# Hybrid decoder step, two layers: input projections on unnormalised activations, and the next layer's splits in the gate loop

## The reference, cut to what matters

```python
def rms_norm(x, w):
    y = x32 * lax.rsqrt(jnp.mean(x32 * x32, axis=-1, keepdims=True) + EPS)
    return y * w

xn = rms_norm(h, norm_pre_mix)
proj = xn @ w_in
hq, hf, hi, hg, aq, ak, av, gq, gk, gv, g_lr, gr = jnp.split(proj, split_points, axis=-1)
...  # HGRN2, GLA (log_a from g_lr @ gla_w_gate2 + gla_b_gate), rotary attention
h = h + rms_norm(mix, norm_post_mix)
h = h + rms_norm(u @ w_down, norm_post_mlp)
h = h + jax.nn.sigmoid(h @ w_ple_gate) * (p_i @ w_ple)
```

## Time and profile before

| | |
|---|---|
| median of 3 runs | 1826.89 us |
| profiled execution, span | 1825.8 us |
| TensorE matmul / weight load | 1719.3 / 1601.2 us busy |
| VectorE / ScalarE / GpSimd | 841.6 / 652.6 / 71.2 us busy |
| DMA | 303.67 MB, mean 166 GB/s |

### The profile page before, as it was taken

How to read it: one execution, slowest core, us unless ns; L and a number is a source line. 1 busy time by engine, 2 the same in 40 slices (tenths; PEclk the granted TensorE clock), 3 DMA queues, 4 the chain that set the end, 5 groups by cost and what they waited for, 6 DMA issues and landing times.

```text
span 1825.8 us, 35764 instructions
## 1 busy us (share of the span) xinstructions
PE 1719.3 (94%) x16070; PEld 1601.2 (88%) x16070; DVE 841.6 (46%) x1311; ACT 652.6 (36%) x963; POOL 71.2 (4%) x90
## 2 busy tenths in 40 slices
PE   6999888899999999999979998888999999999988
PEld 5988775598999999998979887756989999999988
DVE  5413775535413333336554147754364243333365
ACT  5422324544423122233354232254443231322333
POOL 0011110000000000000000121100000000000000
PEclk9999898999999999999989998999999999999999
DMA  6511519931936636442354223398329266355311
GB/s 261 192 58 59 177 53 391 359 136 59 345 105 219 221 100 210 150 150 70 107 180 139 69 89 126 123 378 315 122 88 344 87 222 216 135 174 178 126 59 64
DMA packets 60649, 303.67 MB, mean 166 GB/s; under 512 B 7120, under 2 KB 8784, under 8 KB 58832
## 3 DMA queue, kind: packets, MB, share of 16 engines
q1 hardware_dynamic: 53072, 200.91, 30.8%
q0 software_dynamic: 7424, 100.47, 15.7%
HBM read 290.74 MB, written 111.08 MB: 220 GB/s over the span
## 4 chain that ended last, share of the span: by engine, by line
PE 85%; DVE 8%; ACT 3%; DMA 2%; issue 2%; SPq 0%; DVEq 0%; ACTq 0%
PE pair L1728 15%; PE pair L1730 15%; PE pair L1729 15%; PE pair L764 2%; PE pair L746 2%; PE pair L748 2%; PE pair L747 2%; PE pair L696 2%; PE pair L766 2%; PE pair L768 2%; PE pair L697 2%; PE pair L698 2%; DMA arena<-cv 2%; PE pair L1053 2%; PE pair L1808 2%
## 5 line engine op out<-in xcount | busy, mean ns | idle before, releaser
L1728 PE MATMUL pair<-x_hi_part,w_hi_part 128*128 128x288 f32 x1088 | 322.2, 296 | 2.1 <-DVE tmp L2107 2.1
L1729 PE MATMUL pair<-x_lo_part,w_hi_part 128*128 128x288 f32 x1088 | 321.0, 295 | 0.0
L1730 PE MATMUL pair<-x_hi_part,w_lo_part 128*128 128x288 f32 x1088 | 319.9, 294 | 0.0
L2044 DVE TENSOR_TENSOR w_lo_part<-raw,w_hi_part 128x1024 fp32r<-128x1024 f32 x154 | 188.7, 1225 | 237.9 <-ACT w_hi_part L1895 237.9
L1728 PE MATMUL pair<-u_hi_part,w_hi_part 128*128 128x288 f32 x928 | 274.7, 296 | 0.0
L1729 PE MATMUL pair<-u_lo_part,w_hi_part 128*128 128x288 f32 x928 | 273.8, 295 | 0.0
L1730 PE MATMUL pair<-u_hi_part,w_lo_part 128*128 128x288 f32 x928 | 272.8, 294 | 0.0
L1895 ACT ACTIVATE w_hi_part<-raw 128x1024 fp32r<-128x1024 f32 x154 | 161.9, 1051 | 212.6 <-PE pair L1730 208.3
L1728 PEld LDWEIGHTS pair<-x_hi_part,w_hi_part 128*128 128x128 f32 x1088 | 203.9, 187 | 2.5 <-DVE tmp L2107 2.5
L1730 PEld LDWEIGHTS pair<-x_hi_part,w_lo_part 128*128 128x128 f32 x1088 | 204.9, 188 | 0.0
L1729 PEld LDWEIGHTS pair<-x_lo_part,w_hi_part 128*128 128x128 f32 x1088 | 204.3, 188 | 0.0
(11 more groups left out here) (284 smaller groups left out, 3414.2 us busy)
## 6 DMA issues: line engine op xcount, KB each, us to landing
raw<-w_units SPq DMA_DIRECT2D x210, 512.0 KB, 3.5
ck_out<-ck POOLq DMA_DIRECT2D x16, 3060.0 KB, 14.1
arena<-cv SPq DMA_DIRECT2D x24, 640.0 KB, 9.6
arena<-ck SPq DMA_DIRECT2D x18, 640.0 KB, 10.7
more<-ck SPq DMA_DIRECT2D x18, 640.0 KB, 13.1
tail<-cv SPq DMA_DIRECT2D x18, 640.0 KB, 9.2
h<-ck SPq DMA_DIRECT2D x12, 640.0 KB, 12.7
y_out<-h SPq DMA_DIRECT2D x16, 288.0 KB, 2.1
```

The lines of the kernel that those rows point to most:

```text
L1728: nc.tensor.matmul(out, wh[:, cols], xh[:, k, t], start=n == 0, stop=False)
L1729: nc.tensor.matmul(out, wh[:, cols], xl[:, k, t], start=False, stop=False)
L1730: mm = nc.tensor.matmul(out, wl[:, cols], xh[:, k, t], start=False, stop=n == KT - 1)
L2044: return tt_(dst, src, hi.bitcast(F32), ALU.subtract).then_inc(*up(done, 1))
```

## The change

The products of IN1 and IN2 and of V are taken of h * weight, without RS, and the factor of each token is applied where PSUM is emptied: VectorE evicts IN1 and multiplies by RSP (the new name of RS, in a tile of its own), ScalarE evicts V with a scale for each token from a small tile RSTOK; hg and gr are multiplied in place by GpSimd (`pre_scale`), aq and ak through the rotary tables, which GpSimd multiplies by RSP.

The sum of squares moves on TensorE from ahead of the products to the seventh of their steps (`s == KT - 2`), with five one-column products for RSTOK, and into pair 3. In layer 0 GpSimd squares the tiles instead of ScalarE, while ScalarE and VectorE split them; the startup loads are put in another order. The first two weight units of a layer (`FIRST = 2`) have places of their own and are split outside the layer's queues: for layer 0 between its tiles, for layer 1 in the last two turns of layer 0's gate loop, where the tiles of the new h are split too (`next_hi`, `next_lo`). A tile's remainder lies where h was, so it waits for the store of that tile (`h_saved`, now two semaphores). SP loads units 4 to 7 of a layer ahead of the states, and the reset mask of the scans comes by a load of its own into the arena. The rotary tables are loaded anew for layer 1. At the end of layer 1 no squares are made any more.

Its core:

```diff
+FIRST = 2
+SPLIT = list(range(FIRST, R_PLE)) + list(range(R_UP, UNITS))
...
+            return pair[3 if name == "sum_pre" else 2 if name in APART else Q[name] % 2]
...
+            sp.dma_start(par[:, :], params[0]).then_inc(*up(s_par0, 16))
+            first_unit(0)
+            pair_of_tiles(0)
+            pair_of_tiles(1)
+            first_unit(1)
+            pair_of_tiles(2)
+            pair_of_tiles(3)
+            first_unit(2)
             sp.dma_start(con[:, 0:C_COS], consts[:, 0:C_COS]).then_inc(*up(s_con, 16))
             sp.dma_start(con[:, C_SCALE:C_END], consts[:, C_SCALE:C_END]).then_inc(*up(s_con, 16))
-            sp.dma_start(par[:, :], params[0]).then_inc(*up(s_par0, 16))
-            for i in range(RAW):
-                sp.dma_start(raw_sb[:, i * 1024:(i + 1) * 1024], w_first[0, i * P:(i + 1) * P, :]).then_inc(*up(s_w0[i], 16))
+            first_unit(3)
...
+        def next_hi(act, k):
+            nc.scalar.activation(NH[:, k], H[:, k], ACT.Copy, scale=par[:, W_PRE + k:W_PRE + k + 1]).then_inc(*up(xn_hi, 1))
+        def next_lo(dve, k, at_layer):
+            dve.wait_ge(xn_hi, KT * at_layer + k + 1)
+            nc.vector.scalar_tensor_tensor(NL[:, k], H[:, k], par[:, W_PRE + k:W_PRE + k + 1], NH[:, k].bitcast(F32),
+                                           ALU.mult, ALU.subtract).then_inc(*up(xn_split, 1))
+        def first_hi(act, i, at_layer):
+            act.wait_ge(s_w0[i], 16 * (at_layer + 1))
+            nc.scalar.activation(win_sb[3 + i][:, 0:1024], raw_sb[:, i * 1024:(i + 1) * 1024], ACT.Copy).then_inc(*up(w0_hi, 1))
+        def first_lo(dve, i, at_layer):
+            dve.wait_ge(w0_hi, FIRST * at_layer + i + 1)
+            nc.vector.tensor_tensor(win_sb[3 + i][:, 1024:2048], raw_sb[:, i * 1024:(i + 1) * 1024],
+                                    win_sb[3 + i][:, 0:1024].bitcast(F32), ALU.subtract).then_inc(*up(w0_split, 1))
+        def add_square(dve, k, at_layer, squares):
+            dve.wait_ge(sq_pre, KT * at_layer + k + 1)
+            if k >= 2:
+                dve.wait_ge(acc_pre, (KT - 1) * at_layer + k - 1)
+            nc.vector.tensor_tensor(RSP, squares(0) if k == 1 else RSP, squares(k), ALU.add).then_inc(*up(acc_pre, 1))
+        @block.gpsimd
+        def _(pool):
+            for k in range(KT):
+                if k % 2 == 0:
+                    pool.wait_ge(s_x[k // 2], 16)
+                nc.gpsimd.tensor_tensor(SQ_FIRST[:, k], H[:, k], H[:, k], ALU.mult).then_inc(*up(sq_pre, 1))
+        @block.scalar
+        def _(act):
+            nc.scalar.preload_act_table_set("natural_log_exp_and_others")
+            act.wait_ge(s_par0, 16)
+            for k in range(KT):
+                if k == 0:
+                    first_hi(act, 0, 0)
+                if k % 2 == 0:
+                    act.wait_ge(s_x[k // 2], 16)
+                next_hi(act, k)
+                if k == 3:
+                    first_hi(act, 1, 0)
+        @block.vector
+        def _(dve):
+            dve.wait_ge(s_par0, 16)
+            first_lo(dve, 0, 0)
+            for k in range(KT):
+                dve.wait_ge(sq_pre, k + 1)
+                next_lo(dve, k, 0)
+                if k == 3:
+                    first_lo(dve, 1, 0)
+                if k >= 1:
+                    add_square(dve, k, 0, lambda j: SQ_FIRST[:, j])
...
+                pool.wait_ge(s_rest, 16)
+                if layer > 0:
+                    pool.wait_ge(s_table, 16 * layer)
+                pool.wait_ge(*at(rs_ready, 1))
+                nc.gpsimd.tensor_tensor(con[:, C_COS:C_BIAS].rearrange("p (a t) -> p a t", a=2),
+                                        con[:, C_COS:C_BIAS].rearrange("p (a t) -> p a t", a=2),
+                                        RSP.rearrange("p (a t) -> p a t", a=1).to_broadcast([P, 2, T]), ALU.mult).then_inc(*up(tab_ready, 1))
...
+                def pre_scale(i):
+                    pool.wait_ge(*at(lin_ev, Q[IN2[i]] + 1))
+                    nc.gpsimd.tensor_tensor(proj[IN2[i]], proj[IN2[i]], RSP, ALU.mult).then_inc(*up(pre_scaled, 1))
...
+                def sum_pre():
+                    ps = home("sum_pre")
+                    if layer == 0:
+                        pe.wait_ge(s_con, 32)
+                    pe.wait_ge(acc_pre, (KT - 1) * (layer + 1))
+                    for tt in range(TT + 1):
+                        t = slice(tt * P, (tt + 1) * P) if tt < TT else slice(T - P, T)
+                        nc.tensor.matmul(ps[:, 1, HALF + tt:HALF + tt + 1], RSP[:, t], ONES[:, 0:1], start=True, stop=True)
+                    for half in range(2):
+                        mm = nc.tensor.matmul(ps[:, half, 0:HALF], ONES, RSP[:, half * HALF:(half + 1) * HALF],
+                                              start=True, stop=True)
+                    mm.then_inc(*up(lin_mm, 1))
...
+                    if s == KT - 2:
+                        sum_pre()
                     if s < KT:
-                        pe.wait_ge(*at(x_split, s + 1))
+                        pe.wait_ge(xn_split, KT * layer + s + 1)
                     for u, lag in enumerate(BEHIND):
-                        if s == lag:
-                            pe.wait_ge(*at(w_split, u + 1))
+                        if s == lag and u < FIRST:
+                            if layer > 0:
+                                pe.wait_ge(*at(lin_ev, u - 1))
+                            pe.wait_ge(w0_split, FIRST * layer + u + 1)
+                        elif s == lag:
+                            pe.wait_ge(*at(w_split, u - FIRST + 1))
...
+                if layer > 0:
+                    act.wait_ge(*at(lin_mm, 0))
...
+                A(RSP, RSP, ACT.Exp, scale=-0.5).then_inc(*up(rs_ready, 1))
+                act.wait_ge(*at(rst_ln, 1))
+                A(RSTOK, RSTOK, ACT.Exp, scale=-0.5).then_inc(*up(rst_ln, 1))
                 act.wait_ge(*at(lb_exp, 1))
...
+                def evac(name, factor=None):
+                    dve.wait_ge(*at(lin_mm, Q[name] + 1))
+                    src, dst = home(name)[:, :, 0:HALF], two(proj[name])
+                    ins = tt_(dst, src, two(RSP), ALU.mult) if factor is None else stt(dst, src, factor, two(RSP), ALU.mult, ALU.mult)
+                    ins.then_inc(*up(lin_ev, 1))
...
+                split_w(2)
+                split_w(3)
...
+                evac("hf0")
+                evac("hf1")
+                if layer == 0:
+                    dve.wait_ge(s_con, 32)
+                evac("gq1", con[:, C_SCALE:C_SCALE + 1])
+                split_w(5)
...
+                evac("hq0")
+                split_w(6)
+                split_w(7)
+                dve.wait_ge(*at(lin_ev, Q["hq1"]))
+                evac("hq1")
...
                 for r in range(4):
                     nc.vector.tensor_tensor_scan(B[:, r], RESET, LV[0][:, r], 0.0, ALU.mult, ALU.add).then_inc(*up(b_ready, 1))
+                evac("gq0", 32.0 ** -0.5)
                 split_w(9)
...
                     act.wait_ge(*at(z_used, k + 1))
                     if k >= 3:
-                        act.wait_ge(*at(acc_pre, k - 2))
-                    A(X[:, 0] if k == 0 else SQN[k % 2], H[:, k], ACT.Square).then_inc(*up(sq_pre, 1))
+                        act.wait_ge(acc_pre, (KT - 1) * (layer + 1) + k - 2)
+                    A(RSP if k == 0 else SQN[k % 2], H[:, k], ACT.Square).then_inc(*up(sq_pre, 1))
+                    if k == 0:
+                        act.wait_ge(s_par0, 16 * (layer + 2))
+                    next_hi(act, k)
...
                         split_w(I_GATE + k + SPLITS)
-                        square_new(k - 1)
-                square_new(KT - 1)
+                        if layer + 1 < DEPTH:
+                            square_new(k - 1)
+                    if k >= KT - FIRST and layer + 1 < DEPTH:
+                        first_hi(act, k - KT + FIRST, layer + 1)
+                if layer + 1 < DEPTH:
+                    square_new(KT - 1)
...
+                def next_tile(k):
+                    dve.wait_ge(*at(h_saved[k % 2], 16 * (k // 2 + 1)))
+                    dve.wait_ge(sq_pre, KT * (layer + 1) + k + 1)
+                    next_lo(dve, k, layer + 1)
...
+                    if layer + 1 < DEPTH:
+                        if k >= 2:
+                            add_square(dve, k - 1, layer + 1, squares)
+                            next_tile(k - 2)
+                        if k >= KT - FIRST:
+                            first_lo(dve, k - KT + FIRST, layer + 1)
+                if layer + 1 < DEPTH:
+                    add_square(dve, KT - 1, layer + 1, squares)
+                    next_tile(KT - 2)
+                    next_tile(KT - 1)
```

More of the change, by code:

```diff
@@ L267, in build @@
         LB, OMLB, LBT = small[:, 20:22], small[:, 22:24], small[:, 24:32]
+        RSTOK, RSP = small[:, 32:32 + TT + 1], rsp_sb[:, :]
         pair = [ctx.enter_context(nc.psum_tensor(f"pair{i}", [P, 2, 512], F32)) for i in range(4)]
@@ L314, in build @@
```

(37 more changed lines are left out.)

173 lines of the change are left out of this document (77 added, 96 removed).

## The result

Timed in turn on the same chips, the kernel before took 1824.93 us (median of 19 runs) and the kernel after 1834.71 us (median of 19): a ratio of 1.0058, 95% interval 1.0046 to 1.0071. The change costs 9.8 us by the medians (10.6 by the ratio) where 8.2 were forecast. The profiled execution of after spans 1831.7 us against 1825.8, 5.9 us more.

A forecast was written before the change was run, and what follows sets the result against it. TensorE, busy 94% of the span, was taken as the bound, so its idle time and clock count. Layer 0's +9.8 and layer 1's -1.6 make +8.2 on the 1826.9 us median: 1835.1 us, range 1824.5 to 1841.

The forecast's parts named there:

- layer 0's start: Layer 0's first three products of IN1 end 5.6 us later than before (bounds 4.0 and 8.0).
- gq0 behind the scans: VectorE evicts gq0 late, TensorE waits at gk1: 2.2 us plus 1.7 for the clock, 3.9 per layer.
- z's claim: z's claim no longer stands behind hq0's eviction on ScalarE: -0.4 us per layer (0 to -0.65).
- gr's multiply: GpSimd's pre_scale of gr runs into VectorE's chain of states: +0.7 us per layer (0 to 1.3).
- layer 1's start: Layer 1's first three products end 5.8 us earlier (bounds 4.5 and 7.7), despite 3.4 us idle for unit 1.
- The exclusion: At layer 0's start, VectorE's two-SBUF-input operations and GpSimd's SBUF reads don't overlap: 11.7 and 10.7 us add up.
- the things at nothing: The tables' product, copy_cache(1), V's scale by token and the squares dropped at layer 1's end cost nothing.
- Rival 1: GpSimd and VectorE don't hold each other up at layer 0's start: total -1.5, 1825.4 us; chance 0.14.
- rival 2: gq0's eviction is not late, gk1 begins without a wait: total +0.4, 1827.3 us; chance 0.12.
- rival 3: Layer 1's start gains nothing, TensorE idle at unit 1 and the last tiles: +14.0, 1840.9 us; chance 0.10.
- rival 4: Rival 1 and rival 2 together: total -9.3, 1817.6 us; chance 0.05.

The follow-up runs named there:

- experiment 3: Kernel after with layer 0's first squares made by ScalarE instead of GpSimd: 1830.45 us, ratio 1.0030 to the kernel before.
- experiment 4: Kernel after with a memset in place of each of GpSimd's eight first squares, RSP constant in layer 0; one profiled run, z products begin at 45.82 us.
- experiment 5: Kernel before with its first squares on GpSimd instead of ScalarE; one profiled run, first sum of squares began at 18.38 us instead of 12.33.
- experiment 7: Kernel after with GpSimd's multiply of gr behind the first product with the carried states, both layers: 1828.29 us, ratio 1.0020 to the kernel before.
- experiment 1: Kernel after with gq0's eviction written ahead of the four scans, both layers: 1825.51 us, ratio 1.0007 to the kernel before.
- experiment 2: Kernel before with gq0 evicted by VectorE behind the scans instead of by ScalarE at once: 1837.55 us, ratio 1.0066.

## Why the prediction was right

**The sum, by its terms.** Us against before; what undoing a part gave is from the ratios, the rest from the profiles:

| term | forecast | profile | undone |
|---|---|---|---|
| layer 0's start | +5.6 | +2.6 | |
| gq0 behind the scans, both layers | +7.8 | 5.0 idle, 3.0 clock | 9.3 |
| z's claim, both | -0.8 | -0.5 | |
| gr's multiply, both | +1.4 | 1.3 idle, clock varies | 7 |
| layer 1's start | -5.8 | -6.5 | |

With the undone values where there are any, the terms make 2.6 + 9.3 - 0.5 + 7 - 6.5 = 11.9; the measured difference is 10.6 by the ratio, within what two such ratios leave open (3.5 each). That the forecast of 8.2 came so near was in part luck, since two misses cancelled: 3.0 too much for layer 0's start and some 5.6 too little for gr.

**Layer 0's start: mechanism right, size off.** The exclusion was read from one row, 4.38 for 1.38 us, and experiments 3, 4 and 5 show it. The 2.6 us lie below the term's lower bound of 4.0. Three parts were too large. First, GpSimd's multiply of a tile with itself took 1.33 in the forecast (bounds 1.15 to 1.46). Its first two, before VectorE began, took 2.25 us:

```profile
5.31 2.25 POOL L397 TENSOR_TENSOR x<-h 128x576 f32<-128x576 f32 x2 [4.86 <-DMA h<-x_t]
```

This is from experiment 5's kernel, and after shows the same 2.25 at 7.97: 1.14 us for one and 1.11 from one to the next, just below the lower bound. With two different inputs (`pre_scale`, 576 elements) it took 1.39 to 1.44: the row at 189.72 that the estimate leaned on was a product of two tensors, too. The Trainium skill (GPSIMD Engine Reference, 3.1 Elementwise) gave an estimate of 1.26, between the two. Second, a pair of excluded operations took 1.62 us (12.38 to 14.00), not 1.11 + 0.70: some 0.2 us of each pair overlap after all. Third, the sum of squares inside the products took 1.87 us (34.56 to 36.43), not 2.5; its ten one-column passes, at which no row of before gave a price, took 1.03 of it. The other way went the loads: GpSimd could begin at 7.97, not at 6.6, which put back 0.5 us behind unit 0's split at 7.5. So unit 2's remainder was through at 28.8 instead of 31.7, and z began 3.0 us earlier than forecast. The idle before unit 1 (6.76 us) was the larger one, as the prediction's own working had placed it (23.6, measured 21.0).

**gq0: right.** The scans began at 70.84 and 975.02; TensorE waited 2.40 and 2.64 against 2.2 forecast (1.0 to 2.6, so layer 1 lies at the edge), and behind it lost 1.5 us to the clock. The forecast took 1.7 and, as bound, zero; over the seven profiles with such a wait twelve of fourteen pauses were followed by a slow stretch, and there is none at gk1 in the five profiles without it.

**gr: the step that was mis-sized.** "0.7 per layer (0 to 1.3)" was right for the idle and left the clock out, which I had priced behind pauses of 2 us and more only. An idle that grows from 0.41 to 1.04 us, in a stage of small products, sets off a slow stretch in nine cases of twelve, and none at 0.41. Per layer it cost some 3.5 us by the times, 2.4 by the estimate of experiment 7: four to five times its idle.

**Layer 1: right.** Idle 3.41 us for unit 1's remainder against 3.4, remainder through at 927.18 - 922.40 = 4.8 us behind gate7's sigmoid, against 919.85 - 915.04 = 4.8. Tile 7 and unit 2 were in time behind it, and SP's loads held nothing up. The gain was 6.5 against 5.8, by the shorter sum of squares; besides, the forecast's own terms (919.85 + 17.6 + 1.85 + 2.5) make 941.8 and not 942.1, so it should have read 6.1. The sum for the whole layer in the profile is 0.0 instead of -1.6, since the clock fell there once more, behind z.

**Of the things at nothing**, the tables' product (2.71 us at 41.59) ran beside VectorE's eviction at 42.44, which took 0.76, like those with GpSimd at rest. One SBUF input isn't held up: the trace agrees with the Trainium skill (SBUF — State Buffer, Who interferes with whom), as the prediction cited it.

```profile
41.59 2.71 POOL L717 TENSOR_TENSOR con<-con,rsp 128x1152 f32<-128x1152 f32 x1
```

```profile
42.44 0.76 DVE L1487 TENSOR_TENSOR arena<-pair,rsp 128x576 f32<-128x576 f32 x1 [0.80 <-PE pair L796]
```

The scale by token on V, `copy_cache` and the dropped squares left no trace in TensorE's waits.

**The rivals.** Rival 1 falls by experiments 3 to 5; rival 2 by 1 and 2; rival 3 by the 6.5 us; rival 4 with 1 and 2.

**Open.** Whether the slow stretches behind the z products belong to the new order isn't settled: they stand in 9 of 18 places in the nine profiles with the new order, in 2 of 6 in those with the old. So isn't the part of experiment 2's 12 us above 9.

## To carry to other kernels

A wait that is removed brings back only what no new wait takes. Here a queue order (an eviction written behind 5 us of scans), a 1.4 us multiply on GpSimd beside VectorE's critical chain, and a split placed last in a queue took more than the removed waits gave; each is mended by moving a line or two. Squares and scalings with SBUF inputs did better on ScalarE, or beside VectorE operations that read PSUM, where VectorE's two-input operations were the ones that TensorE waited for. And an idle of TensorE is to be priced with the clock behind it, as a chance: 0.6 us more of idle cost 2.4 to 3.5.

## What the runs showed that was not expected

The price of an idle isn't a function of its length alone. At 2.4 to 2.9 us a slow stretch followed in 12 of 14 cases, at 1.04 us in the stage of small products in 9 of 12, at 0.41 there in 0 of 12; and two profiles of the same kernel differ in four of six places (gk1, behind z, the chain of states, in both layers), with the same idle times there. Single profiles of this kernel can therefore be compared stage by stage in their idle times, but not in their spans: the second profile of after is 3.0 us longer than the first.

GpSimd's multiply of a tensor with itself (1.14 us for 576 elements) is a fifth cheaper than that of two tensors (1.39 to 1.44), and a memset of the same size takes 0.58; of these, only the forms that read held VectorE up.
